# A decoder layer with conv and gating mixer on 8 cores: norm of the mixer applied after the next tile's gating products, x tiles loaded and normalised in another order

## The reference, cut to what matters

```python
def layer(x, p_emb, conv_prev, ...):
    h = x + 0.5 * rmsnorm(swiglu(rmsnorm(x, ffn1_pre_g), ...), ffn1_post_g)      # FFN 1
    n = rmsnorm(h, mix_pre_g)
    b_a, c_a, h_a, u, v = split(n @ w_in)                                        # 5 x 512 columns
    conv_out, new_conv = causal_dwconv(conv_prev, c_a * h_a, conv_w)
    y_a = b_a * conv_out
    v_n = rmsnorm(v per head of 64, v_norm_g)
    mixed = chunk_spatial_mix(v_n, w_s, b_s)                                     # tril(w_s) @ v_n, chunks of 128
    y_b = u * mixed
    y = concat(rmsnorm(y_a, out_g_a), rmsnorm(y_b, out_g_b)) @ w_out
    h = h + rmsnorm(y, mix_post_g)
    h = h + 0.5 * rmsnorm(swiglu(rmsnorm(h, ffn2_pre_g), ...), ffn2_post_g)      # FFN 2
    h = h + rmsnorm(sigmoid(h @ ple_w_gate) * (p_emb @ ple_w_proj), ple_post_g)  # PLE
    return h, new_conv, v_cur
```

## Time and profile before

| | us |
|---|---|
| time before, median | 1377.72 |
| lowest | 1377.32 |
| the profiled execution, own time | 1379.56 |
| its span on the slowest core (core 7) | 1378.5 |
| spans of the cores | 1363.9 to 1378.5 |
| TensorE busy (PE) | 1305.4 (95%) |
| VectorE busy (DVE) | 524.1 (38%) |
| ScalarE busy (ACT) | 415.0 (30%) |
| chain that ended last | PE 84%, DVE 6%, DMA 3%, issue 3%, ACT 3% |

### The profile page before, as it was taken

One profiled execution on the slowest core, in us unless ns is written; L12 is line 12 of the kernel. 1 busy time (PEld: TensorE's weight loads), 2 busy tenths in 40 slices (PEclk: granted clock), 3 DMA queues, 4 the chain that ended last, 5 costly groups with the idle time before them and its releaser, 6 DMA issues.

```text
span 1378.5 us, 18493 instructions; the slowest of 8 cores (1363.9 to 1378.5 us)
## 1 busy us (share of the span) xinstructions
PE 1305.4 (95%) x6710; PEld 647.0 (47%) x6710; DVE 524.1 (38%) x691; ACT 415.0 (30%) x860; POOL 94.3 (7%) x185
## 2 busy tenths in 40 slices
PE   5999999999989999999996999999999899999995
PEld 3566664455445666644441444444444344444442
DVE  2322223356677222213365322223466922221337
ACT  3311112344355111111175111123333721111136
POOL 2100000001000200000010000000010020000000
PEclk8999999999999999999997999999999999999998
DMA  9997422129525963231289974321295297423123
GB/s 215 178 222 154 68 47 46 31 45 183 92 42 82 175 124 62 47 69 25 45 202 211 220 159 87 63 53 31 62 175 107 50 147 141 91 48 68 31 39 122
DMA packets 88185, 139.87 MB, mean 101 GB/s; under 512 B 58272, under 2 KB 58528, under 8 KB 87456
## 3 DMA queue, kind: packets, MB, share of 16 engines
q0 software_dynamic: 25296, 90.25, 39.7%
q1 hardware_dynamic: 62800, 48.43, 13.2%
HBM read 206.03 MB, written 9.51 MB: 156 GB/s over the span
## 4 chain that ended last, share of the span: by engine, by line
PE 84%; DVE 6%; DMA 3%; issue 3%; ACT 3%; POOL 0%; DVEq 0%; ACTq 0%; POOLq 0%; SPq 0%
PE ps L218 56%; PE ps L538 23%; PE ps L527 3%; DMA y<-big 2%; DVE zsc L227 2%; DVE nT L227 1%; DVE big L231 1%; DMA h<-xT 1%; ACT big L223 1%; DVE big L227 1%; DMA ring<-w 1%; ACT nT L223 1%; ACT sg L223 1%; ACT L223 1%; DVE nbr L227 1%
## 5 line engine op out<-in xcount | busy, mean ns | idle before, releaser
L218 PE MATMUL ps<-nT,ring 128*128 128x384 bf16 (+1 forms) x4160 | 785.3, 351 | 18.7 <-DVE nT L227 9.2
L218 PEld LDWEIGHTS ps<-nT,ring 128*128 128x128 bf16 x4160 | 409.7, 99 | 392.3 <-issue 44.0
L231 DVE TENSOR_TENSOR big<-ps,sg 128x384 bf16<-128x384 f32 (+1 forms) x220 | 133.9, 610 | 489.4 <-PE ps L218 479.4
L538 PE MATMUL ps<-ring,big 128*128 128x512 bf16 x1320 | 285.5, 379 | 4.5 <-DVE big L231 4.5
L223 ACT ACTIVATE sg<-ps 128x384 f32<-128x384 f32 (+1 forms) x237 | 127.1, 537 | 506.4 <-PE ps L218 496.8
L538 PEld LDWEIGHTS ps<-ring,big 128*128 128x128 bf16 x1320 | 128.9, 98 | 161.0 <-issue 6.2
L259 POOL DMA_DIRECT2D ring<-w x170 | 89.9, 535 | 1104.5 <-PE ps L218 621.6
L223 ACT ACTIVATE big<-ps 128x1024 bf16<-128x1024 f32 (+4 forms) x88 | 75.4, 870 | 229.4 <-PE ps L538 192.4
L227 DVE SCALAR_TENSOR_TENSOR zsc<-ps,st,gains 128x1024 f32<-128x1024 f32 x51 | 65.4, 1282 | 192.5 <-ACT st L223 192.2
L538 PE MATMUL ps<-ring,nT 128*128 128x512 bf16 x480 | 105.4, 379 | 1.0 <-DVE big L231 1.0
L231 DVE TENSOR_TENSOR big<-ps,big 128x384 f32<-128x384 f32 (+3 forms) x77 | 50.8, 686 | 62.1 <-PE ps L218 34.4
(11 more groups left out here) (63 smaller groups left out, 369.3 us busy)
## 6 DMA issues: line engine op xcount, KB each, us to landing
ring<-w POOLq DMA_DIRECT2D x170, 512.0 KB, 14.5
h<-x SPq DMA_DIRECT2D x17, 512.0 KB, 30.7
y<-big SPq DMA_DIRECT2D x13, 512.0 KB, 10.7
gains<-gain SPq DMA_DIRECT2D x12, 512.0 KB, 9.3
h<-xT SPq DMA_DIRECT2D x3, 1536.0 KB, 13.2
big<-xT SPq DMA_DIRECT2D x2, 2048.0 KB, 20.0
y<-zsc SPq DMA_DIRECT2D x4, 512.0 KB, 12.0
big<-pT POOLq DMA_DIRECT2D x2, 512.0 KB, 7.9
```

The source lines that it names most:

```text
L218: ins = nc.tensor.matmul(out_ap, l, r, start=(i == 0), stop=(i == n - 1))
L231: return DVE.mark(nc.vector.tensor_tensor(out=out, in0=in0, in1=in1, op=op))
L538: ins = nc.tensor.matmul(o.t, lhs(k), sv, start=(k == 0), stop=(k == nk - 1))
```

## The change

It has four parts, and no operation is added but filler matmuls.

1. Start: fill 0 is issued right behind the first memset on POOL, ahead of the mask work; the load of x tile 1 is issued right behind that of tile 0 instead of waiting for fill 0; tile 2 waits for fill 1 as before. Filler matmuls are 120 and 36 instead of 90.
2. Mixer: `norm_tile` is split. `norm_stat(ti - 1)` stays where it was, `norm_apply(ti - 1)` (8 DVE multiplications) moves behind the M instructions; the sum of squares of y_a moves from ahead of the U products to behind the second of them; the buffers of squares are 6 instead of 4.
3. Between the passes: x tile 0 of pass 1 is applied ahead of the last group's PLE products on DVE instead of behind them and their squares.
4. x tile 1 of pass 1: the squares stay behind the first unit, its sum and its application move behind the second unit.

```diff
@@ start
     xt_load(PASSES[0], 0)
     ev_gc = gc_sem.add(nc.sync.dma_start(out=gc_t[:], in_=gcol_d))
+    xt_load(PASSES[0], 1)
     ev_ones = pchain(nc.gpsimd.memset(ones_t[:], 1.0 / 512.0))
+    issue_next()
     pchain(nc.gpsimd.memset(mask_v, 1.0))
...
-    for ti in range(1, 3):
-        xt_load(PASSES[0], ti, [fill_ev[ti - 1][0]])
+    xt_load(PASSES[0], 2, [fill_ev[1][0]])
...
-    for _ in range(90):
-        ins = nc.tensor.matmul(warm.t[:, 0:128], ones_t[:], ones_t[:], start=True, stop=True)
-    warm.free = PE.mark(ins)
+    def warm_up(n):
+        PE.wait(ev_ones, banks[7].free)
+        for _ in range(n):
+            ins = nc.tensor.matmul(banks[7].t[:, 0:128], ones_t[:], ones_t[:], start=True, stop=True)
+        banks[7].free = PE.mark(ins)
+
+    warm_up(120)
...
-    x_apply(PASSES[0], 0, *x_stat(PASSES[0], 0, x_square(PASSES[0], 0), get_bank))
+    first = x_stat(PASSES[0], 0, x_square(PASSES[0], 0), get_bank)
+    warm_up(36)
+    x_apply(PASSES[0], 0, *first)
@@ def mixer
-        sq_free = [conv_all] * 4
+        sq_free = [conv_all] * 6
...
-        def norm_tile(ti, bank_of=get_bank):
+        def norm_stat(ti, bank_of=get_bank):
+            c0, w = P.tiles[ti]
+            par = ti % 2
+            return rstd_bc(*stat(y_ev[ti][1], w, bank_of), zsc_t[:, par, 512:1024], w, rs_free[par])
+
+        def norm_apply(ti, e_b):
             c0, w = P.tiles[ti]
             par = ti % 2
             ra, rb = zsc_t[:, par, 0:512], zsc_t[:, par, 512:1024]
-            ya, yb, ev_u = y_ev[ti]
-            e_b = rstd_bc(*stat(yb, w, bank_of), rb, w, rs_free[par])
+            ya, _, ev_u = y_ev[ti]
...
             if ti >= 1:
-                norm_tile(ti - 1)
+                e_b = norm_stat(ti - 1)
             sqa = []
...
-            e_a = rstd_bc(*stat(sqa, w), zsc_t[:, ti % 2, 0:512], w, rs_free[ti % 2])
+            if ti >= 1:
+                norm_apply(ti - 1, e_b)
             sqb = []
             for c in range(4):
                 b, evl = proj(fU, evU, ti, c)
+                if c == 1:
+                    e_a = rstd_bc(*stat(sqa, w), zsc_t[:, ti % 2, 0:512], w, rs_free[ti % 2])
                 y = mixo[:, c, c0:c0 + w]
...
         def tail():
-            norm_tile(nt - 1, get_tp)
+            norm_apply(nt - 1, norm_stat(nt - 1, get_tp))
@@ def ple
                 del nT_ev[b]
+            if N is not None and gi == 2:
+                xs["ev"] = x_apply(N, 0, *xs["st"])
             zev = {}
...
-            if N is not None and gi == 2:
-                xs["ev"] = x_apply(N, 0, *xs["st"])
             for b in grp:
                 r, e3 = st[b]
@@ pass 1, x tile 1
+    def next_square():
+        nx["sq"] = x_square(PASSES[1], 1)
+
     def next_mid():
-        e = x_apply(PASSES[1], 1, *x_stat(PASSES[1], 1, x_square(PASSES[1], 1), get_bank))
+        e = x_apply(PASSES[1], 1, *x_stat(PASSES[1], 1, nx["sq"], get_bank))
...
-            gu_stage(P, 3, guard1, {(0, 0): (1, next_mid)})
+            gu_stage(P, 3, guard1, {(0, 0): (1, next_square), (1, 0): (1, next_mid)})
```

More of the change, by code:

```diff
@@ L385, in build_program @@
         issue_next()
-    for ti in range(1, 3):
-        xt_load(PASSES[0], ti, [fill_ev[ti - 1][0]])
+    xt_load(PASSES[0], 2, [fill_ev[1][0]])
     act([ev_ones], out=st_t[:, 0, 0:1], in_=ones_t[:, 0:1], func=AF.Ln)
-    warm = banks[7]
-    PE.wait(ev_ones)
-    for _ in range(90):
-        ins = nc.tensor.matmul(warm.t[:, 0:128], ones_t[:], ones_t[:], start=True, stop=True)
-    warm.free = PE.mark(ins)
+    def warm_up(n):
[4 more added lines that the diff above has]
+    warm_up(120)
     const = {}
@@ L576, in mixer @@
         vn = [bigf[:, ZR + 256 * i:ZR + 256 * (i + 1)].bitcast(BF16) for i in range(8)]
-        sq = [bigf[:, ZR + 2048 + 256 * i:ZR + 2304 + 256 * i].bitcast(BF16) for i in range(4)]
+        sq = [bigf[:, o:o + 256].bitcast(BF16) for o in [ZR + 2048 + 256 * i for i in range(4)] + [ZR + 4096, ZR + 4352]]
         gvb = bigf[:, ZR + 3072:ZR + 3584]
@@ L682, in square @@
         def square(src, w, ev):
-            i = cnt["sq"] % 4
+            i = cnt["sq"] % 6
             cnt["sq"] += 1
@@ L899, in start_loads @@
         gain_load(2)
+    nx = {}
+    def next_square():
+        nx["sq"] = x_square(PASSES[1], 1)
     def next_mid():
-        e = x_apply(PASSES[1], 1, *x_stat(PASSES[1], 1, x_square(PASSES[1], 1), get_bank))
+        e = x_apply(PASSES[1], 1, *x_stat(PASSES[1], 1, nx["sq"], get_bank))
         SP.wait(e)
```

## The result

The changed kernel takes 1359.2 us (1358.7 to 1359.5). Against the kernel before the ratio is 0.987, 95% interval 0.984 to 0.989; the kernel before took 1377.5 us beside it, so 18.3 us went. All times here are medians of undisturbed runs.

A forecast was written before the change was run, and what follows sets the result against it. TensorE, busy 95% of the span, was taken as the bound. Terms -4.0, -5.6, -4.8 and -5.7 sum to -20.1, from 1379.56 to 1359.5; with the median 1.8 lower, 1357.6 us, range 1350.5 to 1366.

The forecast's parts named there:

- the 92%: Whole kernel: chance given to a time within 2% (27.6 us) of the kernel before.
- The likeliest case: Whole kernel: all four terms hold, 1357.6 us, bounds 1351 to 1364; chance 55%.
- Start, -4.0: Start of pass 0: squares of x tile 1 begin at 23.3 instead of 27.19, -4.0 us (bounds 0 and -6).
- The premise that tile 0 and fill 0 share evenly: Start: DMA engines alternate between queues, so tile 0 lands at 12.8 us instead of 9.96.
- The rival that tile 0 takes the gain with it (1361.6): Start: tile 0 lands at 14.5, tile 1 at 27, the term is 0; 1361.6 us, chance 15%.
- Mixer, -5.6 and -5.7: Mixer stages of pass 0 and pass 1: PE no longer waits behind the norm, -5.6 and -5.7 us.
- Hole, place and price of the half clock behind it: Mixer, pass 0, ahead of token block 0: PE waits 4.3 us, then 1.7 us charged for half clock.
- Between the passes, -4.8: From pass 0 to pass 1: earlier PE start and stores, no stand at the squares, -4.8 us (bounds 0 and -6.5).
- PE has meanwhile done 104 matmuls where it had done 88: Between the passes: 16 more matmuls done when tile 1's multiplications end, worth 3.5 us.
- The rival that I gave 17%: Between the passes: stores bound by transfer, third lands at 767.3 as before, no gain; 1362.4 us, chance 17%.
- Clock comes back (10%): Mixer, pass 1's first unit and FFN 2: half-clock stretches run at 2.4 GHz, 7 us gained; 1350.6 us, chance 10%.
- the slower rival (3%): Token stage: the new hole keeps PE's clock at 0.50, nine blocks 29 us more; 1387 us, chance 3%.

The follow-up runs named there:

- the pair of runs above: Changed kernel with x tile 1 loaded behind fill 0 again, 1364.2 us; changed kernel with fill 0 issued behind the masks again, 1359.5 us.
- parts 3 and 4 alone: The kernel before with only the two edits between the passes; 1376.1 us, ratio to before 0.9992.
- the fastest kernel: Changed kernel with x tile 1's sum and application half a unit sooner and the first output projection's bank pair chosen for each pass; 1340.3 us, ratio 0.9733.

## Why the prediction was right or wrong, point by point

**The time.** 1357.6 forecast, 1359.2 measured, inside the range, and within 2% of before as the 92% had it. That it lies so near is in part luck. The likeliest case held for three of its four terms; the fourth, 4.8 us, was not there, and the mean core gained 16.0 and not 20.1. The time hides most of that, because the cores also came closer together, which I had not forecast.

**Start, -4.0: right size, by luck in half of the way.** Tile 0 landed at 10.3 in the mean and not at 12.8. Tile 1 landed at 22.7 where I had 22.5, but from two errors that cancel. I let it follow a tile 0 that was 2.5 us too late, and at 0.16 MB/us, because I took the window of the earlier trace rows to hold a whole tile in 9 us. The trace of that core has the load on its way from 13.65 to 27.11, so the window holds two thirds of it, and in the changed kernel tile 1 came in 12.4 us behind tile 0, 0.13 MB/us. And my sum let the Silu, at 23.4, set the squares; in the run it began at 22.0, held by the fill and not by tile 0, and on six of the eight cores the load set them, at 23.1 in the mean. The premise that tile 0 and fill 0 share evenly is refuted by the pair of runs above: 1.1 us of delay, with tile 1 taking most of what the early fill costs (4.8 us). I had drawn that even share of bytes from the packet by packet turn in the Trainium skill, DMA: Bandwidth & Descriptors, "Queues, rings and completion order". The section speaks of packets and not of bytes, and the transfers here were not equal in bytes: with two x tiles queued on SP's side, the first half of the fill, one third of a tile's written bytes, took 15.6 us, and 11.5 with one. The rival that tile 0 takes the gain with it (1361.6) fell.

**Mixer, -5.6 and -5.7: right.** Measured -6.3 and -5.5. Hole, place and price of the half clock behind it stood as forecast. What I had not seen is that the hole was a matter of which bank pair comes first, worth 5.6 us, and 12.6 with the pair chosen for each pass.

**Between the passes, -4.8: the step that failed.** The stage was 0.4 us shorter in the changed kernel, and with parts 3 and 4 alone the mean core moved by 0.1. Three of its numbers were off. "PE starts at about 739.6 ... not at 740.30": no gain, 48.2 us behind FFN 2's last block before and after. "Issued 5.3 us earlier ... landed at 762.0 if the latency holds": the issue came 4.5 us earlier (50.7 against 55.2 us behind FFN 2's last block, mean of the cores), and the first product that waits for a store came 12.1 behind that issue instead of 10.8, so 3.2 of the 5.3 were left at the first store. The multiplications behind the third then start 24.7 us after PE does, where 23.3 had been measured before and my numbers gave 23.4. And "PE has meanwhile done 104 matmuls where it had done 88": it has, but eight of them at the pace of DVE, at the price of the clock, which I had counted only for holes. The rival that I gave 17%, stores bound by the transfer, had the better mechanism and the right outcome, an even stage, though the stores did land sooner. Three of the nine stores, core 6 of the changed kernel, issued at 729.16, 731.69 and 734.21 (KB, us to landing):

```profile
y<-big SPq DMA_DIRECT2D x1, 512.0 KB, 11.9
y<-big SPq DMA_DIRECT2D x1, 512.0 KB, 14.5
y<-big SPq DMA_DIRECT2D x1, 512.0 KB, 16.4
```

They are issued 2.5 us apart and land 4.4 to 5.2 apart. In the mean of the cores all nine stores of the changed kernel land 4.6 to 4.9 us behind one another, which fits stores that are bound by the transfer. In the kernel before the seventh landed 8.5 us behind the sixth: there the queue had a gap. If so, the 3.2 us were all that an earlier issue could give at the first of these stores; at the third 2.6 were left. I had treated parts 3 and 4 as one step; apart, they are -3.5 and +3.

**Clock comes back (10%) and the slower rival (3%).** Neither: the stretches at half clock behind the hole, at the start and between the passes stayed, and the token stage kept DVE's pace. TensorE's mean granted clock on the slowest core went from 0.976 to 0.983, and to 0.990 in the fastest kernel, where the holes ahead of the token stages are gone.

## What to carry to other kernels

When work is moved behind another instruction in an engine's queue, write down every wait that now stands ahead of it: the two evictions that part 4 put ahead of the norm carried a wait for a store, and turned a good edit into a loss. Look at each edit of a change alone, also where they touch one stage. And where an engine waits for a PSUM bank, ask first whether another bank is free: starting the rotation elsewhere, with no instruction moved, brought 12.6 us where the whole change had brought 18.3. Last, put the mean over the cores beside the time of the slowest: only there did the parts of this change add up.

## What the runs showed of the hardware

- A transfer issued early lands early by less, or not at all. The first half of fill 0, issued 2.8 us sooner, landed 1.3 us sooner with two x tiles queued beside it (17.5 against 18.8) and no sooner with one (13.4 against 13.3). It delayed the x tile under way by 1.1 us and the one queued behind it by 4.8. The stores of y, issued 4.5 us sooner, landed 3.2 sooner, at the 4.6 to 4.9 us for 512 KB that the queue kept throughout.
- A consumer at the pace of its producer can lose its clock without standing still for long. Paced at 0.66 us a matmul behind a wait of 0.99 us, PE fell to a granted clock of 0.51 (754.2 to 761.0), which cost some 1.9 us once its work no longer waited; after one stop of 1.40 us it ran on at 1.00.
- The spread between cores that run the same program (2 to 15 us over the executions of the kernel before, 3.5 to 5.6 after) is large enough to be mistaken for an effect when a forecast is made on the slowest core alone. The mean over the cores stayed within about 2.5 us from one execution to the next.
